# A second layer's residual stream kept with features on partitions: no transposes of x3 and x4

## What is computed

```python
# first block, its last steps (x2 is the residual before the FFN)
x3 = x2 + einsum('bsf,fd->bsd', silu(gate) * up, w_down)     # f = 2816, d = 1024
x  = rms_norm(x3, final_norm_gain)
# second block
h = rmsnorm(x, norm1_g);  proj = h @ w_in_2                  # 3*512 hyena + 512 fourier columns
y = head_rmsnorm(concat([hyena_mixer(...), fourier_mixer(...)]), mix_g)
x4 = x + y @ w_out_2
h  = rmsnorm(x4, norm2_g)
logits = h @ [w_group, w_router] + bias                      # 36 columns, top-1 group, top-2 of 8 experts
x5 = x4 + moe(h)                                             # 32 experts, each 3 x 1024 x 512 weights (6 MB)
out = rmsnorm(x5, final_g)
```

## Time and profile before

| | |
|---|---|
| median of 3 runs | 1051.56 us (1049.44 to 1051.91) |
| profiled execution, first to last instruction | 1050.5 us |
| TensorE busy | 923.8 us (88%) |
| VectorE busy | 510.8 us (49%) |
| ScalarE busy | 238.6 us (23%) |
| HBM read | 287.17 MB |

### The profile page before, as it was taken

How to read it: one execution, slowest core, us unless ns; L and a number is a source line. 1 busy time by engine, 2 the same in 40 slices (tenths; PEclk the granted TensorE clock), 3 DMA queues, 4 the chain that set the end, 5 groups by cost and what they waited for, 6 DMA issues and landing times. The chain is left out here.

```text
span 1050.5 us, 19577 instructions
## 1 busy us (share of the span) xinstructions
PE 923.8 (88%) x8288; PEld 618.3 (59%) x8288; DVE 510.8 (49%) x1283; ACT 238.6 (23%) x498; POOL 4.7 (0%) x11
## 2 busy tenths in 40 slices
PE   9999999999999999999999987976767776677686
PEld 7986467764499999644696445543334433343343
DVE  4894546578785555568568474321222212221122
ACT  2015223462221111000311232312121121221213
POOL 0100000000000000000000000000000000000000
PEclk9999999999999999999999999988888888888889
DMA  9744420035244444753165879999999999999995
GB/s 370 295 175 162 160 83 2 1 153 206 109 169 161 161 170 179 297 195 111 49 265 235 350 304 402 424 434 430 428 427 434 435 428 429 427 432 435 429 426 223
DMA packets 22839, 289.03 MB, mean 275 GB/s; under 512 B 2688, under 2 KB 4480, under 8 KB 8192
## 3 DMA queue, kind: packets, MB, share of 16 engines
q1 hardware_dynamic: 22784, 288.23, 67.1%
HBM read 287.17 MB, written 1.05 MB: 274 GB/s over the span
## 5 line engine op out<-in xcount | busy, mean ns | idle before, releaser
L463 PE MATMUL ps<-sb_ring,sb_own 128*32 128x256 f32 x1936 | 154.1, 480 | 104.8 <-DMA sb_ring<-w_exp 101.3
L463 PEld LDWEIGHTS ps<-sb_ring,sb_own 128*32 128x32 f32 x1936 | 80.1, 137 | 176.7 <-issue 108.0
L2898 DVE TENSOR_TENSOR sb_own<-sb_own,ps 128x128 f32<-128x128 f32 x32 | 9.2, 288 | 310.6 <-ACT sb_own L1950 310.6
L1281 PE MATMUL ps<-sb_nsa,sb_ring 128*128 128x128 f32 x640 | 74.7, 275 | 0.0
L1281 PEld LDWEIGHTS ps<-sb_nsa,sb_ring 128*128 128x128 f32 x640 | 73.1, 192 | 0.0
L483 PE MATMUL ps<-sb_ring,sb_own 128*32 128x256 f32 (+1 forms) x1024 | 60.4, 375 | 4.1 <-DVE sb_own L2898 2.7
L1961 ACT ACTIVATE sb_own<-ps 128x256 f32<-128x256 f32 x32 | 12.3, 385 | 208.5 <-PE ps L463 208.5
L1281 PE MATMUL ps<-sb_hT,sb_ring 128*128 128x128 f32 x480 | 56.9, 275 | 0.0
L1281 PEld LDWEIGHTS ps<-sb_hT,sb_ring 128*128 128x128 f32 x480 | 55.3, 192 | 0.1
L814 PE MATMUL ps<-sb_ring,sb_hT 128*128 128x512 f32 (+1 forms) x128 | 50.6, 550 | 0.0
L483 PEld LDWEIGHTS ps<-sb_ring,sb_own 128*32 128x32 f32 x1024 | 30.7, 109 | 30.0 <-issue 10.7
(11 more groups left out here) (605 smaller groups left out, 1504.3 us busy)
## 6 DMA issues: line engine op xcount, KB each, us to landing
sb_ring<-w_exp SPq DMA_DIRECT2D x26, 4096.0 KB, 23.5
sb_ring<-w_exp SPq DMA_DIRECT2D x38, 2048.0 KB, 22.6
sb_ring<-w_in SPq DMA_DIRECT2D x13, 2048.0 KB, 8.4
sb_ring<-w_gu SPq DMA_DIRECT2D x11, 2048.0 KB, 8.0
sb_ring<-w_dn SPq DMA_DIRECT2D x10, 1024.0 KB, 6.9
sb_ring<-w_out SPq DMA_DIRECT2D x4, 2048.0 KB, 7.8
sb_ring<-w_branch SPq DMA_DIRECT2D x2, 2048.0 KB, 8.7
sb_ring<-cmp_w SPq DMA_DIRECT2D x1, 2048.0 KB, 8.3
```

Source lines behind the costliest of these rows:

```text
L463: m = pe.matmul(ps[group(j), 2, 0:256], hgT[:, k, :], w[j // 2][k][:, (j % 2) * 256:(j % 2 + 1) * 256], start=(k == 0), stop=(k == KT - 1))
L1281: m = pe.matmul(out[:, i, :], w[:, k, i * P:(i + 1) * P], h[:, k, :], start=start and i == 0 and k == 0, stop=(k == KT // 2 - 1), skip_gro ...
```

## The change

The residual of the second layer is kept with features on partitions from x2 on: `xT` is the same memory as `x`, seen as 8 tiles of 128 features x 256 tokens.

- Down: the operands change sides. The stationary operand is a 128x128 block of the weights (or of their sums), the moving one the 128 tokens of the gated activation, so a product is four matmuls of 128 columns instead of one of 512. The seven-product scheme is written anew for the turned blocks; VectorE's sums have the same sizes.
- x2 is copied turned into `xT` by ScalarE (four copies of 128x512 out of PSUM) behind the copy of the x2 scale.
- x3: no transposes. VectorE multiplies `xT` by the gain straight into `hT` in two halves (`h3_out`). The norm sums go over partitions now, so they are made by TensorE: ScalarE squares `xT`, `column_sums` multiplies the squares by `total_weights` (16 columns of ones, 16 of squared final gains) in four column groups, ScalarE copies the result, `row_totals` adds the groups per token. These stand between the halves of the Fourier projection.
- Two scales are spread instead of one (L1484 in the kernel after): the mixer's, and the root with which POOL multiplies the residual, after ScalarE has multiplied it by the final gain (eight ACTIVATEs of 128x256 between the x1 and the Fourier copies).
- Output projection: the weights are stationary, 256 tokens move; 64 matmuls of 256 columns instead of 32 of 512. A unit u is two feature tiles.
- Router: `logits_part(u)` and `x4_sums(u)` follow the units as they become ready and stand between the last units of the projection. The logits product has 256 columns per tile. The token scale comes out of `row_totals` and a ScalarE Sqrt. `take_x` turns x4 back (16 matmuls of 128 columns) before the routing decisions are awaited; the two `keep_clock` matmuls between logits and ranks are gone (those further on stay). The normed rows for the gather are read from PSUM by ScalarE.
- SP: the load into `hT` moves up to behind `conv_made`, the load into `x` waits for `x_taken` alone; the first spare load waits also for `residual_ready`.

The diff at its core:

```diff
@@ down
-                terms = {1: (g[:, 0, TOK[0]], w[:, 0, 0]), 2: (g[:, 1, TOK[0]], w[:, 1, 0]), 3: (gs[:, 3], w[:, 1, 1]),
-                         4: (g[:, 1, TOK[1]], ws[:, 3]), 5: (gs[:, 0], ws[:, 0]), 6: (gs[:, 1], ws[:, 1]), 7: (gs[:, 2], ws[:, 2])}
+                terms = {1: (w[:, 0, 0], g[:, 0, TOK[0]]), 2: (w[:, 1, 0], g[:, 1, TOK[0]]), 3: (ws[:, 3], g[:, 1, TOK[1]]),
+                         4: (w[:, 1, 1], gs[:, 3]), 5: (ws[:, 0], gs[:, 0]), 6: (ws[:, 1], gs[:, 1]), 7: (ws[:, 2], gs[:, 2])}
...
-                    m = pe.matmul(ps[:, SUM_BANK[j], :], *terms[j], start=(n == 0), stop=(n == N_FC - 1), skip_group_check=True)
+                    left, right = terms[j]
+                    for i in range(4):
+                        m = pe.matmul(ps[:, SUM_BANK[j], i * P:(i + 1) * P], left[:, i * P:(i + 1) * P], right,
+                                      start=(n == 0 and i == 0), stop=(n == N_FC - 1), skip_group_check=True)
@@ x3 on TensorE
-            for b in range(NB):
-                pe.wait_ge(sig("x3_step"), b + 1)
-                for half in range(2):
-                    transposes(4 + 2 * b + half, [x[:, b, (4 * half + n) * P:(4 * half + n + 1) * P] for n in range(4)], "x3_turned")
+            def column_sums(bank, weights_of, squared, tiles):
+                for k in tiles:
+                    m = pe.matmul(ps[quarter(k % 4), bank, 0:T], weights_of(k), squared(k), start=(k < 4), stop=(k >= 4))
+                return m
+            def row_totals(bank, right):
+                n = right.free_size()
+                for b in range(NB):
+                    m = pe.matmul(ps[:, bank, T + b * n:T + (b + 1) * n], partial_sums[:, b * P:(b + 1) * P], right, start=True, stop=True)
+                return m
...
+            project_fourier(0, 0)
+            pe.wait_ge(sig("x3_squared"), 2)
+            column_sums(7, lambda k: total_weights[:, k, :], lambda k: squares_x3[:, k, :], range(KT)).then_inc(sig("x3_summed"), 1)
+            project_fourier(0, 1)
+            pe.wait_ge(sig("x3_sums_ready"), since("x3_sums_ready", 1))
+            row_totals(7, cols[:, C_TOTAL:C_TOTAL + 2]).then_inc(sig("x3_totals_made"), 1)
+            for half in range(2):
+                project_fourier(1, half)
@@ output projection and router on TensorE
-                        m = pe.matmul(ps[:, 4 + 2 * b + half, :], src[:, k % NHT, b * P:(b + 1) * P], w[:, k, :],
+                        for i in range(2):
+                            at = (2 * (u % 2) + i) * P
+                            m = pe.matmul(ps[:, 4 + u, i * T:(i + 1) * T], w[:, k, at:at + P], src[:, k % NHT, :],
...
+            last_mixed(0)
+            last_mixed(1)
+            logits_part(0)
+            last_mixed(2)
+            x4_sums(0)
+            logits_part(1)
+            last_mixed(3)
+            x4_sums(1)
+            logits_part(2)
+            x4_sums(2)
+            logits_part(3).then_inc(sig("logitsT_made"), 1)
+            x4_sums(3).then_inc(sig("x4_sums_made"), 1)
...
-            take_x(range(2))
-            keep_clock(2)
+            take_x(range(4)).then_inc(sig("x_taken"), 1)
+            pe.wait_ge(sig("logits_read"), since("logits_read", 1))
@@ ScalarE, before the routing
+            for u in range(4):
+                act.wait_ge(sig("x4_summed"), since("x4_summed", u + 1))
+                act.activation(square_x4(u).rearrange("p (k t) -> p k t", t=T), xT[:, 2 * u:2 * u + 2, :], ACT.Square).then_inc(sig("x4_squared"), 1)
+            act.wait_ge(sig("logitsT_made"), since("logitsT_made", 1))
+            act.activation(logitsT.rearrange("p b t -> p (b t)"), ps[:, 0, 0:T], ACT.Copy).then_inc(sig("logitsT_ready"), 1)
+            act.wait_ge(sig("x4_totals_made"), since("x4_totals_made", 1))
+            act.activation(stat[:, 0:NB], ps[:, 1, T:T + NB], ACT.Sqrt, ...).then_inc(sig("row_root"), 1)
@@ VectorE, x4
+            dve.wait_ge(sig("residual_ready"), 2)
+            for u in range(4):
+                dve.wait_ge(sig("out2_made"), since("out2_made", u + 1))
+                at = xT[:, 2 * u:2 * u + 2, :]
+                dve.tensor_tensor(at, at, ps[:, 4 + u, :].rearrange("p (k t) -> p k t", t=T), ALU.add).then_inc(sig("x4_summed"), 1)
+            dve.wait_ge(sig("x4_sums_made"), since("x4_sums_made", 1))
+            dve.tensor_copy(partial_sums, ps[:, 1, 0:T]).then_inc(sig("x4_sums_ready"), 1)
@@ POOL
+            pool.wait_ge(sig("residual_gained"), since("residual_gained", 1))
+            pool.wait_ge(sig("scales_ready"), since("scales_ready", 1))
+            for half in range(2):
+                at = xT[:, 4 * half:4 * half + 4, :]
+                pool.tensor_tensor(at, at, spread(mix_root, 1, 4), ALU.mult).then_inc(sig("residual_ready"), 1)
```

More of the change, by code:

```diff
@@ L527, in two_layer_program @@
         block = ctx.enter_context(nc.Block())
-        SIDES = [(half, b) for half in range(2) for b in range(NB)]
         IN2_SLOTS, OUT2_SLOTS = (3, 4, 5, 1), (0, 2)
@@ L708, in _ @@
             load_spare(1, 6, 8, silu_z.rearrange("p b n -> p (b n)"))
+            sp.wait_ge(sig("conv_made"), since("conv_made", 2))
+            sp.dma_start(hT_flat, down[:, 0:4 * BANK]).then_inc(sig("spare_down_loaded"), 16)
             sp.wait_ge(sig("hy_normed"), since("hy_normed", 4))
@@ L1429, in inverse_transform, with project_mixed @@
                 m.then_inc(sig("conv_made"), 1)
-            def project_mixed(banks, tiles, src, first, last):
-                for b, half in banks:
-                    mix_weights(OUT2_SLOTS[half])
-                    w = ring[:, OUT2_SLOTS[half], :].rearrange("p (k n) -> p k n", n=BANK)
+            def project_mixed(units, tiles, src, first, last):
+                for u in units:
+                    mix_weights(OUT2_SLOTS[u // 2])
+                    w = ring[:, OUT2_SLOTS[u // 2], :].rearrange("p (k n) -> p k n", n=BANK)
@@ L1506, in _ @@
             pe.wait_ge(sig("hy_normed"), since("hy_normed", 4))
-            for half, b in SIDES:
-                project_mixed([(b, half)], range(2, 4), y_hy, False, True).then_inc(sig("out2_made"), 1)
-            for n, (half, b) in enumerate(SIDES):
-                    pe.wait_ge(sig("x4_summed"), n + 1)
-                    transposes(2 * half + b, [x[:, b, (4 * half + n) * P:(4 * half + n + 1) * P] for n in range(4)], "x4_turned")
-            for b in range(NB):
-                for half in range(2):
-                    if b == 0:
-                        pe.wait_ge(sig("h4_scalar"), half + 1)
-                    else:
-                        pe.wait_ge(sig("h4_ready"), since("h4_ready", half + 1))
-                    for k in range(4 * half, 4 * half + 4):
-                        m = pe.matmul(ps[64 * (k % 2):64 * (k % 2) + 64, 5 - b, 0:P], route_tile(k), hT[:, k, b * P:(b + 1) * P],
-                                      start=(k < 2), stop=(k >= KT - 2))
-                m.then_inc(sig("logitsT_made"), 1)
@@ L1524, in _, with last_mixed, logits_part @@
-            for b in range(NB):
-                pe.wait_ge(sig("logitsT_ready"), since("logitsT_ready", b + 1))
-                m = pe.matmul(ps[:, 6, b * N_LOG:(b + 1) * N_LOG], logitsT[:, b, :], cols[:, C_PICK:C_PICK + N_LOG], start=True, stop=True)
+            def last_mixed(u):
+                project_mixed([u], range(2, 4), y_hy, False, True).then_inc(sig("out2_made"), 1)
+            def logits_part(u):
+                pe.wait_ge(sig("x4_summed"), since("x4_summed", u + 1))
+                for k in (2 * u, 2 * u + 1):
+                    m = pe.matmul(ps[64 * (k % 2):64 * (k % 2) + 64, 0, 0:T], route_tile(k), xT[:, k, :], start=(k < 2), stop=(k >= KT - 2))
+                return m
@@ L1530, in take_x @@
             def take_x(quarters):
                 for q in quarters:
-                    m = pe.matmul(ps[:, 4 + q, :], ident, x[:, :, q * Q_COLS:(q + 1) * Q_COLS], start=True, stop=False, skip_group_check=True)
+                    for b in range(NB):
+                        for i in range(2):
+                            m = pe.matmul(ps[:, 4 + q, b * T + i * P:b * T + (i + 1) * P], xT[:, 2 * q + i, b * P:(b + 1) * P], ident,
+                                          start=(b == 0 and i == 0), stop=False, skip_group_check=True)
@@ L1852, in _ @@
             act.activation(wide_scale, ps[:, 2, 0:T], ACT.Copy).then_inc(sig("x2_wide_ready"), 1)
+            act.wait_ge(sig("x2_turned"), since("x2_turned", 4))
+            act.wait_ge(sig("x2_squared"), since("x2_squared", 2))
+            for b, half in X2_ORDER:
+                act.activation(x_block(half, b), as_block(ps[:, X2_BANK[b, half], :]), ACT.Copy).then_inc(sig("x2_copied"), 1)
             act.wait_ge(sig("plain_scaled"), 1)
@@ L1893, in main_copies @@
                     act.activation(mixed_home(first, half, b), mixed_out(banks[0]), ACT.Copy).then_inc(sig(copied), 1)
-            act.wait_ge(sig("x3_step"), 4)
             main_copies("x1")
+            act.wait_ge(sig("h3_ready"), since("h3_ready", 2))
```

(3 more changed lines are left out.)

221 lines of the change are left out of this document (105 added, 116 removed).

## The result

| | before | after |
|---|---|---|
| median of the runs | 1050.94 us (4 runs, 1049.44 to 1051.91) | 1057.62 us (4 runs, 1056.54 to 1059.31) |
| profiled execution, first to last instruction | 1050.5 us | 1054.3 us |
| restart of the expert loads | 619.56 us | 626.26 us |

The forecast was 1055.5, range 1051.4 to 1058.8. The time lies in that range, but above 1054.2 to 1057.2, which the prediction calls the forecast's own. The difference is larger than the forecast's 3.9 us, and the two profiled spans differ by only 3.8. Both have to be explained.

What follows compares the result with a forecast made beforehand. TensorE's chain until expert 3's loads restart at 619.56 us, then the full-rate weight stream, bounds the kernel. 2.7 - 0.3 + 0.3 + 1.3 = +4.0 (3.9 unrounded) on 1050.5 gives 1054.4, plus 1.06: 1055.5; range 1051.4 to 1058.8, own 1054.2 to 1057.2.

Steps and rivals of the forecast that it cites:

- Down +2.7: Down products: 616 records of 128 columns at 0.1117 us take 68.8 us instead of 66.10, without cover, +2.7 us.
- x3 and Fourier -0.3: x3 and Fourier projection: transposes gone, column groups, row totals and two more scale matmuls added; together -0.3 us (-0.8 to +0.6).
- What is hidden: x2 copies, small VectorE operations, gain ACTIVATEs (3.0 us), POOL's two products and the Fourier half of the output projection cost nothing.
- Output projection and router +0.3 and +1.3: Hyena half of the output projection 14.0 us instead of 13.7, +0.3; router from projection's end to logits 5.97 instead of 4.70, +1.3.
- the 0.50 for a group: Router: each of eight small groups of two matmuls taken at 0.50 us, near the 0.55 of one alone; 4.0 in all.
- From the logits to the gather: VectorE's list unchanged, `take_x` (3.6 us) and ScalarE's PSUM reads covered, so no cost; without cover about 1 us.
- Rival (c): TensorE's clock falls around the ranks, nearly idle about 2.5 us before and 2.3 behind: +3.2 on top, 1058.7; chance 0.12.
- the prediction's own last paragraph: Wrong if restart differs from TensorE's terms, end does not follow restart, or clock is below 1.00 before the first expert.
- What makes the first expert's gate and up products later or earlier by some time makes the end later or earlier by the same time: Expert 3's loads restart when those products end, at 619.56 us; delays pass to the end one to one, nothing given back.
- The median of the runs lies 1.06 us above that span: Added 1.06 us to the forecast span of 1054.4, from the profiled 1050.5, to get a time of 1055.5.
- Sum: 2.7 - 0.3 + 0.3 + 1.3 = +4.0 us (3.9 unrounded) on the profiled span of 1050.5; own range +2.6 to +5.6.
- Rival (d): Weight loads not hidden in down: pitch could double, 69 us more, 1123; chance 0.01.

Runs made afterwards that it cites:

- The profile with the 1.92 us stretch: The kernel before without its two unread matmuls between logits and ranks, all of `take_x` ahead of the ranks: 1052.70 us beside 1051.94, ratio 1.0006.

## Why the prediction was right or wrong

- **Down +2.7**: right, 2.69, shown alone. **x3 and Fourier -0.3**: measured -0.05 with all up to the output projection, inside the bounds. The 16 column-group records took 1.00 instead of 0.86, the projection in its three pieces 14.02 instead of 13.81 (start to start), and the row totals 0.36 instead of 0.45; the four scale records more were 0.44, as said.
- **What is hidden**: right. The gain ACTIVATEs took 3.29 us in a gap (the first Fourier copy follows x1 by 13.57 us in both kernels), and POOL's two products 5.00, off the path. The Trainium skill ("GPSIMD Engine Reference", "4.1 Engine selection") had given an estimate of 2 x 2.3, and the trace about agrees:

```profile
530.96 5.00 POOL L805 TENSOR_TENSOR sb_x<-sb_x,sb_nsa 128x1024 f32<-128x1024 f32 x2 [30.77 <-ACT sb_x L1955]
```

- **Output projection and router +0.3 and +1.3**: a size was off. It was +2.15 (20.69 against 18.54). The eight groups took 4.57 us, 0.57 each, instead of 8 x 0.50; the projection's records 14.4 (18.96 to L1576 less 4.57) instead of 14.0, where they had been 13.84 and not 13.7 before; the tail to the logits 1.73 instead of 1.97. The step that failed is the 0.50 for a group: the value nearest to hand, the group alone at 0.55, was the right one, and the discount for neighbours was not there.
- **From the logits to the gather, "covered"**: this step failed. It holds for VectorE (+0.07), but it priced only what stands in TensorE's list and put the clock at nothing in the sum. Rival (c), at 0.12, is what happened on top of the forecast. It said +3.2; measured 1.3 and 2.8. What spoke against it, "the rank matmuls lie between", did not hold it off: they are in the 0.9 us of work. The 3.36 us of idleness at 1.00 were no sign of safety: 5.35 us with 0.9 us of work in them are followed by 0.50. By the prediction's own last paragraph, a clock below 1.00 before the first expert is a sign that it is wrong, and it was seen.
- **"What makes the first expert's gate and up products later or earlier by some time makes the end later or earlier by the same time"**: right (+2.7 at the restart gave +2.6 in the time, +4.1 gave +3.9). It looked wrong in the two profiles because the first profile of before had lost about 2 us behind its restart.
- **"The median of the runs lies 1.06 us above that span"**: this step failed. A run's time is 2.2 us above its own span; the profiled execution lost about 2 us in an idle stretch, and the two partly cancelled: the base of 1051.56 was 0.6 us above the 1050.94 of the comparison. The row that gave it away was used only as evidence on the clock: the idle stretch at 644.91 whose releaser is "issue".
- **Sum.** 2.69 - 0.05 + 2.15 + 0.07 + 1.25 = 6.1 us in the first profile, 7.6 with the longer fall of the clock, against 6.7 and 7.1 between the medians. The forecast of 3.9 missed about 0.6 in the output projection and router and 1.3 to 2.8 in the clock. The time came out 2.1 us above 1055.5 and not 2.8 only because the base was 0.6 us too high, which is luck. It lies in the range because that was drawn up to rival (c), and (c) is what came: the sum by itself, with its own 1054.2 to 1057.2, fell short.
- **Rival (d)'s 1123** adds its 69 us to the span of 1054.4; added to the time it is 1124. Down at 68.79 us rules it out.

## What to carry to other kernels

Removing unread matmuls, or moving real ones away from a place where TensorE waits, can change the clock there: compare what stays in the idle stretches, not only the instruction's own cost. Before a profile serves as the base of a sum, look for idle stretches that nothing in the profile releases, and take the time from events (restart plus a stretch that is the same everywhere) rather than from one span. Here four column-group records in two groups took 0.57 us and eight in four groups 0.57 as well, so it pays to fill all four groups. And where a rival comes with a priced term, as (c) did, ask which row holds it off before leaving it out of the sum.

## What the runs showed of the hardware that was not expected

- TensorE's code comes by the same 16 DMA engines as the weights, in 16 KB packets (queue "q8 instruction"). In three profiles such a packet came 15.9 to 17.7 us behind the restart instead of 12.9 or less, and TensorE then stood idle for 1.9 to 3.4 us. 154 instructions that do nothing, put where issue has spare time, took the spread of spans from 3.9 us to 1.8, and with halved loads from 4.5 and 6.5 us to 1.1. That the late packet is the cause of the idleness rests on its times and on this shift; no run delayed a packet by itself.
- The same code in the same order had the clock at 0.50 for 3.4 us in one execution and for 6.0 in another. What makes the difference stays open.
- The MB left at a given time behind the restart agree within 0.2 in the nine profiles of kernels with whole loads and no such idle stretch, with restarts from 619.37 to 627.53 us. The profile with the 1.92 us stretch (restart 622.10) has 0.3 to 0.4 MB more left from +36 us on.
